# A two-layer diffusion backbone on one core: the modulation maps of layer 0 split in a first group and the rest

## The reference, cut to what matters

```
def _modulation(cond, w_mod, b_mod):      # silu(cond) @ w_mod + b_mod, split in 6
x_mod = x * (1.0 + scale) + shift         # before the mixer, parts 0 (shift) and 1 (scale)
z = x_mod @ w_in                          # layer 0: 1024 x 2464, the input projection
```

## Time and profile before

| | us |
|---|---|
| median of 3 runs | 2101.63 (2097.73 to 2106.29) |
| the profiled execution | 2110.22 |
| its span, first to last instruction | 2108.7 |
| TensorE busy, matmul | 1719.4 (82%) |
| VectorE, ScalarE, POOL busy | 673.7, 340.3, 310.4 |
| DMA moved | 592.37 MB, mean 281 GB/s |
| granted TensorE clock, mean | 0.877 of 2.4 GHz |

### The profile page before, as it was taken

One profiled execution on the slowest core, in us unless ns is written; L12 is line 12 of the kernel. 1 busy time (PEld: TensorE's weight loads), 2 busy tenths in 40 slices (PEclk: granted clock), 3 DMA queues, 4 the chain that ended last, 5 costly groups with the idle time before them and its releaser, 6 DMA issues. The chain is left out here.

```text
span 2108.7 us, 19654 instructions
## 1 busy us (share of the span) xinstructions
PE 1719.4 (82%) x7040; PEld 886.1 (42%) x7040; DVE 673.7 (32%) x1271; ACT 340.3 (16%) x767; POOL 310.4 (15%) x228
## 2 busy tenths in 40 slices
PE   3649788966999996889887678986999969898875
PEld 0117647734544432333332466744443423333322
DVE  0014244767432211111112846385422111111117
ACT  0004153000111110111111215301111101111120
POOL 0000000121121111323310320031111113211110
PEclk8769887576899998999998789887999989999997
DMA  9974001033799999999996501217899999999965
GB/s 371 430 300 149 32 11 41 6 125 130 287 364 403 412 412 403 416 393 408 396 393 272 184 11 41 94 62 311 317 398 415 401 393 404 405 389 387 378 256 239
DMA packets 109396, 592.37 MB, mean 281 GB/s; under 512 B 22672, under 2 KB 24720, under 8 KB 55664
## 3 DMA queue, kind: packets, MB, share of 16 engines
q1 hardware_dynamic: 85680, 540.70, 63.6%
q0 software_dynamic: 23616, 50.38, 6.2%
HBM read 578.23 MB, written 48.41 MB: 297 GB/s over the span
## 5 line engine op out<-in xcount | busy, mean ns | idle before, releaser
L2000 PE MATMUL bank<-weights,scratch 128*64 128x512 f32 x448 | 219.1, 646 | 90.8 <-DMA scratch<-in_moe_w_up 46.6
L2105 DVE TENSOR_TENSOR scratch<-scratch,bank 128x256 f32<-128x256 f32 x88 | 53.9, 613 | 678.7 <-ACT scratch L2074 649.8
L2001 PE MATMUL bank<-scratch 128*64 128x512 f32 x480 | 234.4, 645 | 0.0
L2000 PEld LDWEIGHTS bank<-weights,scratch 128*64 128x64 f32 x448 | 64.3, 149 | 234.7 <-issue 234.7
L2000 PE MATMUL bank<-scratch 128*64 128x512 f32 x288 | 133.7, 619 | 20.4 <-DMA scratch<-in_moe_w_up 20.4
L2074 ACT ACTIVATE scratch<-bank 128x256 f32<-128x256 f32 x88 | 33.9, 385 | 713.5 <-PE bank L2001 436.3
L2006 PE MATMUL bank<-weights,scratch 128*128 128x512 f32 x320 | 141.9, 596 | 2.1 <-ACT scratch L2069 1.7
L2001 PE MATMUL bank<-weights,scratch 128*64 128x512 f32 x256 | 119.1, 620 | 0.0
L2006 PE MATMUL bank<-scratch 128*128 128x512 f32 x256 | 112.9, 594 | 0.0
L1806 POOL DMA_INDIRECT y_rows<-hP,y_idx x42 | 43.5, 1037 | 466.4 <-DVE hP L2110 385.7
L2033 PE MATMUL bank<-scratch 128*64 128x512 f32 x240 | 109.4, 598 | 0.0
(11 more groups left out here) (315 smaller groups left out, 2767.4 us busy)
## 6 DMA issues: line engine op xcount, KB each, us to landing
weights<-in_moe_w_gate SPq DMA_DIRECT2D x64, 1024.0 KB, 11.3
weights<-in_moe_w_up SPq DMA_DIRECT2D x64, 1024.0 KB, 18.2
weights<-in_moe_w_down SPq DMA_DIRECT2D x64, 1024.0 KB, 20.3
scratch<-in_moe_w_gate SPq DMA_DIRECT2D x64, 1024.0 KB, 11.5
scratch<-in_moe_w_up SPq DMA_DIRECT2D x64, 1024.0 KB, 20.8
scratch<-in_moe_w_down SPq DMA_DIRECT2D x64, 1024.0 KB, 18.5
wmod_more<-in_w_mod SPq DMA_DIRECT2D x9, 3072.0 KB, 31.7
weights<-in_w_mod SPq DMA_DIRECT2D x7, 3072.0 KB, 32.2
```

The costliest lines, as they stand in the source:

```text
L2000: nc.tensor.matmul(out[0:HALF, :], x[:, 0:HALF], w0[:, kk], start=(kk == 0), stop=(kk == KT - 1))
L2001: m = nc.tensor.matmul(out[HALF:P, :], x[:, HALF:P], w1[:, kk], start=(kk == 0), stop=(kk == KT - 1))
L2105: nc.vector.tensor_tensor(B.h[b % 2].rearrange("p (j q) -> p q j", j=2), B.ex[b % 2].rearrange("p (q j) -> p q j", j=2), k.ps[2 + b % 2][: ...
```

## The change

`stage_setup`, `stage_mod` and `stage_modulate` go; two stages take their place and that of layer 0's projection.

`stage_first_mod` multiplies only columns 0 to 2047 of layer 0 (shift and scale), in four pieces of 2048 KB (256 of the 1024 rows each, all 2048 columns, two runs of 8 KB per partition), into bank 7. x and the tables are loaded over ScalarE's queue; x is turned as it is, before it is modulated. The map row is turned too (four turns), so that shift and scale stand as one value per partition, and the modulation is one instruction per 128 channels and condition: four channel groups on ScalarE, four on VectorE, straight into hT. SP then loads w_in's chunks 0 and 1 and piece 4.

`stage_project_beside_mod` does layer 0's projection with two ring slots for chunks and three half-chunk buffers for `w_hi` and `w_lo`, tile by tile as before but with the three passes done for the first half of the rows and then for the second. Between the tiles TensorE multiplies the other 20 map pieces (five groups of four, 2048 columns each, banks 6 and 7 by turns): piece 4 first, then after tile b all pieces up to (b+1)*20/15. They come into two slots. The group's row is added to its bias by VectorE; POOL loads the bias and stores the row. Layer 1 keeps `stage_project`.

```diff
+MOD_COLS = 4 * 512
+MOD_PIECES = KT // 2
+def mod_piece(k, n):
+    group, part = divmod(n, MOD_PIECES)
+    layer, c = mod_group(group)
+    return k.io["w_mod"][layer].rearrange("(p k) n -> p k n", k=KT)[:, 2 * part:2 * part + 2, c:c + MOD_COLS]
+def pe_mod_piece(k, n, bank, w):
+    part = n % MOD_PIECES
+    for kk in range(2):
+        for j in range(4):
+            m = k.nc.tensor.matmul(k.ps[bank][32 * j:32 * j + 32, :], k.cond[:, 2 * part + kk, :], w[:, kk, 512 * j:512 * (j + 1)],
+                                   start=(n % MOD_PIECES == 0 and kk == 0), stop=(part == MOD_PIECES - 1 and kk == 1))
+    return m
...
+def stage_first_mod(k, w):
...
         @blk.sync
         def _(sp):
             sp.dma_start(craw[:, 0, :], io["c_ctx"].rearrange("(p k) -> p k", k=KT)).then_inc(s_c, 16)
             sp.dma_start(craw[:, 1, :], io["c"].rearrange("b (p k) -> p (b k)", k=KT)).then_inc(s_c, 16)
+            for n in range(MOD_PIECES):
+                sp.dma_start(slots[n], mod_piece(k, n)).then_inc(s_w[n], 16)
+            first_chunks(k, w, 2)(sp)
+            k.load_ahead(sp, 2, piece_view(k.ring[:, 8192:12288]), mod_piece(k, MOD_PIECES))
 
         @blk.scalar
         def _(act):
+            act.dma_start(k.x[:, 0, :], io["x_prompt"].rearrange("b s d -> (b s) d")).then_inc(s_x, 16)
+            act.dma_start(k.x[:, 1:3, :], io["x_sample"].rearrange("b (t p) d -> p (b t) d", p=P)).then_inc(s_x, 16)
+            act.dma_start(k.const[:], io["tables"]).then_inc(k.s_const, 16)
...
+            for b in range(0, 2 * TILES, 2):
+                act.wait_ge(s_tr, b + 1)
+                nc.scalar.copy(xT[:, 0:4, b // 2 * P:(b // 2 + 1) * P], k.ps[b][:].rearrange("p (j n) -> p j n", j=4)).then_inc(s_xa, 1)
+            act.wait_ge(s_xa, TILES)
+            act.wait_ge(s_cols, 2)
+            for kk in range(4):
+                for r, lo, hi in ((0, 0, P), (1, P, TOK)):
+                    m = nc.scalar.activation(k.hT[:, kk, lo:hi], xT[:, kk, lo:hi], ACT.Identity, bias=turned[:, 0, kk, r:r + 1],
+                                             scale=turned[:, 2, kk, r:r + 1])
...
+            nc.vector.tensor_tensor(rows, k.ps[7][:], bias, ALU.add).then_inc(s_row, 1)
+            dve.wait_ge(s_rt, 1)
+            nc.vector.tensor_copy(cols, k.ps[6][:]).then_inc(s_cols, 1)
...
+            for kk in range(4, KT):
+                for r, lo, hi in ((0, 0, P), (1, P, TOK)):
+                    nc.vector.tensor_scalar(k.hT[:, kk, lo:hi], xT[:, kk, lo:hi], turned[:, 3, kk - 4, r:r + 1], turned[:, 1, kk - 4, r:r + 1],
+                                            ALU.mult, ALU.add)
...
+            piece(0)
+            pe.wait_ge(s_x, 32)
+            pe.wait_ge(k.s_const, 16)
+            for b in range(2 * TILES):
+                for j in range(4):
+                    kk = 4 * (b % 2) + j
+                    m = nc.tensor.transpose(k.ps[b][:, j * P:(j + 1) * P], k.x[:, b // 2, kk * P:(kk + 1) * P], k.ident)
+                m.then_inc(s_tr, 1)
+            for n in range(1, MOD_PIECES):
+                m = piece(n)
+            m.then_inc(s_mm, 1)
+            pe.wait_ge(s_row, 1)
+            for c in range(4):
+                m = nc.tensor.transpose(k.ps[6][:, c * P:(c + 1) * P], rows[:, c * P:(c + 1) * P], k.ident)
+            m.then_inc(s_rt, 1)
...
+def stage_project_beside_mod(k, w, n_cols, out):
...
+        x_hi, x_lo = sb("x_hi", [P, KT, TOK], F32R), sb("x_lo", [P, KT, TOK], F32R)
+        w_hi, w_lo = sb("w_hi", [P, 3, KH, 512], F32R), sb("w_lo", [P, 3, KH, 512], F32R)
+        more = sb("wmod_more", [P, 2 * MOD_COLS], F32)
+        slots = [piece_view(k.ring[:, 8192:12288]), piece_view(more[:])]
...
+            def piece(n):
+                i = n - MOD_PIECES
+                if i == 0:
+                    return
+                if i >= 2:
+                    sp.wait_ge(s_mod, i - 1)
+                sp.dma_start(slots[i % 2], mod_piece(k, n)).then_inc(s_ml[i % 2], 16)
+
+            for n in pieces:
+                i = n - MOD_PIECES
+                if i % MOD_PIECES == 2 and i // MOD_PIECES + 2 < N:
+                    j = i // MOD_PIECES
+                    c, m = chunks[j + 2]
+                    sp.wait_ge(s_wl, 2 * (j + 1))
+                    sp.dma_start(ring_slot(k, j % 2)[:, :, 0:m], w.rearrange("(k p) n -> p k n", p=P)[:, :, c:c + m]).then_inc(s_w[j % 2], 16)
+                piece(n)
...
+            for g in groups:
...
+                for r in range(2):
+                    pool.dma_start(bias[r:P:32, :], mod_strips(io["b_mod"][layer], c)).then_inc(k.s_bias, 16)
+                pool.wait_ge(s_row, g)
+                for r in range(2):
+                    pool.dma_start(mod_strips(k.mod_d[layer, r], c), rows[r:P:32, :]).then_inc(k.s_mod_out, 16)
+            pool.wait_ge(k.s_mod_out, 32 * N)
...
+            piece(0)
+            done = 1
+            for i, (c, n) in enumerate(chunks):
+                for t in range(TILES):
+                    b = i * TILES + t
+                    if b >= BANKS:
+                        pe.wait_ge(s_v if b % 2 else s_a, (b - BANKS) // 2 + 1)
...
+                    m.then_inc(s_mm, 1)
+                    upto = (b + 1) * len(pieces) // (N * TILES)
+                    for p in range(done, upto):
+                        piece(p)
+                    done = upto
...
+        def buffer_free(eng, q):
+            if q >= 3:
+                eng.wait_ge(s_mm, TILES * ((q - 3) // 2 + 1))
...
+            def mod_rows(g):
+                dve.wait_ge(s_mod, MOD_PIECES * g)
+                dve.wait_ge(k.s_bias, 32 * g)
+                if g > 1:
+                    dve.wait_ge(k.s_mod_out, 32 * (g - 1))
+                nc.vector.tensor_tensor(rows, k.ps[6 + (g - 1) % 2][:], bias, ALU.add).then_inc(s_row, 1)
...
+            for i in range(N):
+                if i + 1 < N:
+                    rest_w(2 * i + 2)
+                for t in range(TILES):
+                    if t == TILES - 1 and i + 1 < N:
+                        rest_w(2 * i + 3)
+                    copy(nc.vector.tensor_copy, dve, s_v, 1, TILES * i + t)
+                if i:
+                    mod_rows(i)
+            mod_rows(N)
...
         k = Kernel(nc, ctx, io)
-        stage_setup(k)
-        stage_mod(k)
         k.work_memory(ctx)
+        stage_first_mod(k, w_in(0))
         for layer in range(DEPTH):
             w_out = io[("even_w_out", "swa_w_out")[layer % 2]][layer // 2]
-            if layer == 0:
-                stage_modulate(k, layer, first_chunks(k, w_in(0)))
```

More of the change, by code:

```diff
@@ L256, in stage_setup, with piece_view @@
+def piece_view(v):
+    return v.rearrange("p (k n) -> p k n", k=2)
+def stage_first_mod(k, w):
     nc, io = k.nc, k.io
+    xT = k.hP[:].rearrange("p t d -> p (t d)").rearrange("p (k n) -> p k n", k=KT)
+    slots = [piece_view(k.s[:, i * 4096:(i + 1) * 4096]) for i in range(MOD_PIECES)]
+    bias, rows, cols = (k.z[:, i * 512:(i + 1) * 512] for i in range(3))
+    turned = cols.rearrange("p (c j r) -> p j c r", c=4, j=4)
     with Stage(nc) as ctx:
-        s_x, s_one = sems(nc, ctx, "x_loaded ones_set")
@@ L259, in stage_setup @@
-        blk = ctx.enter_context(nc.Block())
[L261 to L271, removed]
@@ L274, in stage_mod @@
[L274 to L302, removed]
+        craw, ce = (k.z[:, 1536 + i * 2 * KT:1536 + (i + 1) * 2 * KT].rearrange("p (r k) -> p r k", r=2) for i in range(2))
@@ L307, in _ @@
             sp.dma_start(craw[:, 1, :], io["c"].rearrange("b (p k) -> p (b k)", k=KT)).then_inc(s_c, 16)
[L308 to L322, removed]
@@ L334, in _ @@
         @blk.gpsimd
         def _(pool):
-            nc.gpsimd.memset(bias[:], 0.0).then_inc(s_zero, 1)
+            nc.gpsimd.memset(bias, 0.0).then_inc(s_zero, 1)
         @blk.vector
@@ L340, in _ @@
             st = Steps(dve, s_d)
-            st.mark(nc.vector.memset(cond[:], 0.0))
+            st.mark(nc.vector.memset(k.ones[:], 1.0))
+            st.mark(nc.vector.memset(k.cond[:], 0.0))
             dve.wait_ge(s_e, 1)
[L343 to L350, removed]
+            st.then(nc.vector.tensor_scalar(ce, ce, 1.0, None, ALU.add))
+            st.then(nc.vector.reciprocal(ce, ce))
+            nc.vector.tensor_tensor(k.cond[:, :, 0:2].rearrange("p k r -> p r k"), craw, ce, ALU.mult).then_inc(s_silu, 1)
@@ L352, in _ @@
         @blk.tensor
         def _(pe):
+            def piece(n):
+                pe.wait_ge(s_w[n], 16)
+                return pe_mod_piece(k, n, 7, slots[n])
             pe.wait_ge(s_silu, 1)
[L355 to L364, removed]
+            piece(0)
@@ L367, in table_load @@
+            m.then_inc(s_rt, 1)
 def table_load(k, eng, sem, out, layer, cond, part):
     eng.dma_start(out, k.mod_d[layer, cond:cond + 1, part * D:(part + 1) * D].to_broadcast([P, D])).then_inc(sem, 16)
[L372 to L388, removed]
-            for t in range(TILES):
-                pe_turn_tile(k, pe, t, (2 * t, 2 * t + 1), s_h, s_tr)
-        @blk.scalar
```

(12 more changed lines are left out.)

143 lines of the change are left out of this document (133 added, 10 removed).

## The result

| | before | after |
|---|---|---|
| median, us | 2102.0 (2097.7 to 2106.3) | 2047.7 (2045.0 to 2052.4) |
| ratio | | 0.9744 (0.9717 to 0.9771) |
| span of the profiled execution | 2108.7 | 2050.8 |
| norm stage starts (ScalarE's square sum of z) | 246.70 | 189.29 |
| from there to the end of the span | 1862.0 | 1861.5 |

The change takes 54.4 us off, 2.6%; 75.3 were forecast, and the time lies 1.7 us above the range. All of it was won where it was looked for: the norm stage starts 57.4 us earlier, and what follows lasts as long as before (1862.0 and 1861.5 us; 1855.8 and 1857.7 in two more traces of the changed kernel, so this rest differs by some us from trace to trace). So the miss has one place, the new projection stage: it was to be over at 171.4 us.

The account below looks back on a forecast made before the run. Map stage bound by DMA, layer 0's projection by TensorE, one behind the other; merged, DMA's 110.3 us exceeds TensorE's 95.9. With queue gaps and tail the stage ends at 171.4 against 246.7: -75.3, 2026.3 us, range 2012 to 2046.

Parts of the forecast that it names:

- TensorE's price of a piece: Projection stage: a map piece of two quads costs TensorE 0.87 us at the fast clock, 1.7 at the slow.
- My own walk: Projection stage, piece by piece through two slots: last piece landed 165.1, used 166.0, its rows added 166.7 us.
- the charges for the slow clock in rounds 3 to 5: Projection stage: 1.7 us added to one tile in each of these rounds, for the clock falling after stalls.
- The front: Before the projection stage: pieces 0 to 3, modulation done by 39.6 us, casts by 45.2, piece 4 landing at 46.3.
- The tail: Projection stage's end: POOL's stores of the last group's rows, wake-ups and barrier take 4.7 us, between 3.7 and 6.
- Waits of TensorE for pieces: Projection stage: TensorE waits 15.8 us in all over five rounds, most at two adjacent pieces behind a third tile.
- the signs: What would show it: among others, DMA share over 0.9 from 2 to 150 us, granted clock over 0.9 from 55 us.
- POOL's round: Projection stage: POOL's four issues and two landings per round take 12.6 us under load, within 25.
- Rival 1: Map pieces go at the rate of lone loads, 6.1 us each: -56.4 us, 2045 us; chance 0.08.
- Rival 2: TensorE's clock stays at half in the projection stage, tiles 10.9 us: -5 us, 2097 us; chance 0.05.
- Rival 3: Loads not overlapped with tiles, each of 19 pieces waited for whole, 7.9 us: +50, 2152 us; chance 0.03.
- Rival 4: POOL's rows hold VectorE and so the casts, four rounds losing up to 10 us: -35, 2066 us; chance 0.04.

Follow-up runs that it names:

- Half loads: Changed kernel, each projection-stage piece but the first loading 1024 KB, that half multiplied twice: norm stage starts at 173.7 us; other routing.
- half the products: Changed kernel with one quad of products instead of two per projection-stage map piece: norm stage starts at 178.7 us, ratio 0.9716, other routing.
- no small rows: Changed kernel with all bias rows loaded at the stage's start and sums stored by four DMAs at its end: norm stage starts at 188.3 us, ratio 0.9719.

## Why the prediction was wrong

**The step that failed: TensorE's price of a piece.** "A quad takes 0.13 + 0.30 = 0.43 us" took the weight-load row of four records as four products. It is half of them. The group at 134.31 in the same rows has 24 records, and the text beside it says that such a load is three times four products: twelve. A float32 product stands as two records, so a quad is eight, 0.86 us at the fast clock, and a piece of eight products is 1.72 us, 1.86 with the change from and to the projection's products. One division in the rows on record would have shown it, and so would another: TensorE was busy 66.89 us from 22 to 134.5, some 4.5 us for each of 15 loads, where this price gives 1.3 at the fast clock and 2.6 at the slow one. TensorE's sum then is not 95.9 us but 12 x 5.70 + 3 x 4.7 + 20 x 1.86 = 120 (from the changed kernel's trace), more than the DMA's 110.3, and the bound changes sides. Half loads measured this floor: 120 us. The three doses of products show the price at work: the norm stage starts at 178.7 with half of them, 183.2 to 189.3 with all, 207.9 with twice as many.

**What the pieces of the miss are.** My own walk, with only the price put right, ends its last row add at 177.6 instead of 166.7 us: 10.9 us (the 7 us in the expectation for half the products leave out the charges for the slow clock in rounds 3 to 5 as well). The three tiles of rounds 3 to 5 that I had charged with the slow clock ran at the fast one in the traces: -3.8. Piece 0 of the stage landed at 47.5, not 46.3: 1.2. A tile beside pieces takes 5.70 instead of 5.44 us: 1.8 in the walk. Together they give 176.8 for the row add, with its tail 181.5 for the norm stage; the three traces of the changed kernel have 184.5, 178.4 and 183.2. The rest, 2 to 8 us, differs from trace to trace: no pieces at the slow clock after piece 0 in the second trace and two in each of the others (1.3 to 1.6 us each), and a last load that took 8.2 to 10.2 us from issue to use instead of 7.7. Half the products, which end 7.3 us late at nearly the forecast's price, point at the same part. That this stage ends 6 us apart from trace to trace was not in my bounds at all.

**Right.** The point at which all is decided, and that nothing behind it changes beyond the spread of traces. The front: pieces 2 and 3 were used at 25.75 and 30.76, 5.0 us apart as priced; the modulation of the turned x ended at 38.9 against "39.6 at the latest"; the stage's first product waited for its first piece, and its casts were ready. There two errors met: the 1.7 us for two quads at the slow clock were half the price (3.47 us in the second trace), but in the first trace the clock was at 2.4 GHz and the piece took 1.93. The tail: 4.8 us against 4.7. Waits of TensorE for pieces: 10.7 us against 15.8, most of it at the stage's pieces 7, 11 and 19, which are three of the walk's. From 2 to 150 us the DMA share was 0.94, from 55 to 150 us the clock 0.98, as the signs asked. No new wait of VectorE, ScalarE or SP came onto the path, and POOL's rows cost nothing that the traces can tell. Three sums on record are a little off, and nothing hung on them: the casts end at 39.6 + 5.2 = 44.8 and not 45.2 us, the chunk of 1664 KB takes 4.4 and not 4.5 us at 388 GB/s, and POOL's round with two landings of 8.6 us is 21 and not 12.6 us, still under its 25.

**The rivals.** Rival 1 gave 2045 us, almost the measured time, by another mechanism, and that mechanism is out: queued pieces come 5.0 us apart, at the front (25.75, 30.76) and in the stage itself (96.41, 101.38). That its time was nearly met is luck: a price on the other engine made up for it. Rival 2 (half clock throughout) did not come: the clock is 1.00 in every window from 60 us but for single pieces. After one and the same wait of 3.0 us in the stage the clock was low in two of three traces, after the same 3.08 us ahead of piece 3 at the front in one of three, and without interleaving it was low at the first piece of every pair, after waits of 2.7 to 5.7 us. The Trainium skill (TensorE: Matmul & The Clock Gate, HAM oscillation) says that a loop that waits for DMA starts each round cold. The traces bear out a part of that: it was so without interleaving, and only at single pieces with it. Rival 3 did not come: TensorE waited 0.6 us a piece, not 5.3, and even without any interleaving the norm stage starts at 242, not 297. Rival 4's stalls did not come either: TensorE waited for nothing but pieces, with POOL's small rows and without them. The range's upper end was set by rival 1 and had no term for TensorE's own sum, since I held it 14 us below the DMA's; a bound on that price from the 24-record row would have widened it.

## What to carry to other kernels

When work moves from a stage where an engine is idle to one where it is busy, its price on that engine becomes the price of the change, and it has to be taken from a row whose record count is matched with the code's instruction count first. Where the two sums come out close together (120 and 110 us here), neither alone gives the end: waits for single loads come on top. Cutting the pieces smaller with as many more slots took most of those waits away (8.3 to 10.7 us down to 3.3); an earlier start did not (8.9). In a balanced stage repeat the trace, on the same chip, before reading differences under 6 us.

## What the runs showed of the hardware

That a float32 product stands as two records in the trace, on which the forecast stumbled; the projection's products, of the rounded type, stand as one. And how a lone load ends: the last piece, issued at 170.32, moves at 391 to 399 GB/s from 174 to 177 us, and then the DMA share falls to 0.42, 0.27 and 0.09 in the three us before it is used. By these shares some seven, four and one or two of the sixteen engines were still at work (an estimate), and the piece waited for them. The length of this end differs: in the second trace of the changed kernel the shares were 0.42 and 0.04, and the load took 8.2 us from issue to use instead of 10.2. Without interleaving the nine loads at the head of a pair took 7.4 to 7.8 us, but for two that took 9.0.

```profile
175.00:176.00 1.00, 1.00 (x12) 0.28 (x12) 0.00 (x0) 0.48 (x1) 0.00 (x0) 1.00 1.03 393
177.00:178.00 1.00, 0.00 (x0) 0.00 (x0) 0.00 (x0) 0.00 (x0) 0.00 (x0) 1.00 0.42 172
178.00:179.00 1.00, 0.00 (x0) 0.00 (x0) 0.00 (x0) 0.00 (x0) 0.00 (x0) 1.00 0.27 115
179.00:180.00 1.00, 0.00 (x0) 0.00 (x0) 0.00 (x0) 0.00 (x0) 0.00 (x0) 0.90 0.09 33
```

It is so with POOL's small rows and without them ("no small rows": issue 169.3, use 179.38, shares of 0.44, 0.18 and 0.06 at the end), so these are not the cause; which engines are late, and why, stays open.
